# A hybrid mLSTM + Mamba-2 + MoE step on one core: decay exponents moved to ScalarE, a tenth weight slot

## What is computed

```python
def ssd_chunk_scan(x, dt, A, bm, cm, S, chunk):          # the 16 SSD heads
    a = jnp.cumsum(dtc * A[:, None], -1)
    decay = jnp.exp(jnp.where(causal, a[..., :, None] - a[..., None, :], -jnp.inf))
    scores = jnp.einsum('bhtn,bhsn->bhts', cc, bc) * decay * dtc[..., None, :]
    y = jnp.einsum('bhts,bhsp->bhtp', scores, xc) + ...

def hier_moe(x, p):                                      # 16 experts, 12 MB of weights each
    hg = jnp.einsum('sd,edf->sef', xr, p['w_gate'])
    hu = jnp.einsum('sd,edf->sef', xr, p['w_up'])
    return jnp.einsum('sef,efd->sd', jax.nn.silu(hg) * hu * gr[..., None], p['w_down'])
```

## Time and profile before

| what | value |
|---|---|
| median of 3 runs | 798.01 us (796.15 to 798.03) |
| time of the profiled execution | 795.37 us |
| its span in the profile | 793.6 us |
| busy in the span | PE 755.2, DVE 288.3, ACT 213.0, POOL 29.9 us |
| DMA | 263.68 MB, 332 GB/s over the span |
| GB/s in slices of 19.8 us, from 357 us to 754 us | 420 to 433 in each |

### The profile page before, as it was taken

How to read it: one execution, slowest core, us unless ns; L and a number is a source line. 1 busy time by engine, 2 the same in 40 slices (tenths; PEclk the granted TensorE clock), 3 DMA queues, 4 the chain that set the end, 5 groups by cost and what they waited for, 6 DMA issues and landing times.

```text
span 793.6 us, 9613 instructions
## 1 busy us (share of the span) xinstructions
PE 755.2 (95%) x3789; PEld 403.7 (51%) x3789; DVE 288.3 (36%) x699; ACT 213.0 (27%) x598; POOL 29.9 (4%) x90
## 2 busy tenths in 40 slices
PE   6998999998999999999999999999999998998995
PEld 5876888876788887533333333333333332233232
DVE  3943555779989311430031031211300201311204
ACT  4226666738564101611100101001011001001013
POOL 7000000001000100000000000000000000000000
PEclk9999999998999999999999999999999999999998
DMA  9954467756796687779999999999999999999992
GB/s 237 340 186 126 130 211 233 239 186 175 249 294 192 271 321 314 281 287 429 426 429 424 433 420 431 427 423 431 424 429 425 427 425 430 427 427 427 427 399 80
DMA packets 76491, 263.68 MB, mean 332 GB/s; under 512 B 7398, under 2 KB 46570, under 8 KB 62856
## 3 DMA queue, kind: packets, MB, share of 16 engines
q1 hardware_dynamic: 74656, 259.02, 83.6%
q0 software_dynamic: 1568, 3.91, 1.4%
q10 hardware_dynamic: 216, 0.07, 0.1%
HBM read 251.15 MB, written 11.99 MB: 332 GB/s over the span
## 4 chain that ended last, share of the span: by engine, by line
PE 73%; DMA 15%; DVE 7%; ACT 2%; issue 1%; POOL 1%; DVEq 0%; POOLq 0%; ACTq 0%
PE bank L2309 21%; PE bank L1886 10%; PE bank L2388 10%; PE bank L2159 7%; DMA arena<-in_w_down 5%; DMA arena<-in_w_up 5%; DMA ring<-in_w_up 4%; PE bank L1874 4%; PE bank L2334 4%; PE bank L2268 3%; PE bank L1973 2%; DVE h_tok L1425 2%; PE bank L1833 1%; PE bank L2322 1%; PE bank L2278 1%
## 5 line engine op out<-in xcount | busy, mean ns | idle before, releaser
L2309 PE MATMUL bank<-ring,arena 128*64 128x512 f32 x704 | 159.2, 596 | 5.4 <-DMA ring<-in_w_up 3.9
L1886 PE MATMUL bank<-arena,ring 128*128 128x264 f32 (+1 forms) x448 | 110.9, 403 | 5.5 <-DVE arena L1564 2.0
L2309 PEld LDWEIGHTS bank<-ring,arena 128*64 128x64 f32 x704 | 47.9, 137 | 102.4 <-issue 91.0
L1886 PEld LDWEIGHTS bank<-arena,ring 128*128 128x128 f32 x448 | 85.8, 195 | 22.6 <-issue 3.9
L512 DVE COPY arena<-bank 64x512 f32<-64x512 f32 x15 | 10.3, 683 | 205.4 <-PE bank L2388 205.4
L2388 PE MATMUL bank<-ring,arena 128*64 128x512 f32 x304 | 68.1, 593 | 3.0 <-DMA ring<-in_w_down 3.0
L1751 DVE TENSOR_TENSOR arena<-bank,WG 128x512 f32<-128x512 f32 x16 | 16.9, 1056 | 129.7 <-PE bank L2309 129.7
L2159 PE MATMUL bank<-arena,ring 128*128 128x264 f32 x256 | 58.4, 387 | 0.0
L2309 PE MATMUL bank<-arena 128*64 128x512 f32 x240 | 55.6, 598 | 2.0 <-DMA arena<-in_w_up 1.2
L2159 PEld LDWEIGHTS bank<-arena,ring 128*128 128x128 f32 x256 | 48.3, 190 | 8.5 <-issue 0.3
L1218 ACT ACTIVATE arena<-bank 128x512 f32<-128x512 f32 x15 | 9.0, 598 | 148.0 <-PE bank L2322 148.0
(11 more groups left out here) (390 smaller groups left out, 807.4 us busy)
## 6 DMA issues: line engine op xcount, KB each, us to landing
ring<-in_w_gate SPq DMA_DIRECT2D x22, 2048.0 KB, 25.2
ring<-in_w_up SPq DMA_DIRECT2D x22, 2048.0 KB, 28.7
ring<-in_w_down SPq DMA_DIRECT2D x19, 2048.0 KB, 27.4
arena<-in_w_down SPq DMA_DIRECT2D x11, 2048.0 KB, 30.9
ring<-in_w_in SPq DMA_DIRECT2D x9, 2048.0 KB, 9.2
arena<-in_w_up SPq DMA_DIRECT2D x5, 2048.0 KB, 25.5
arena<-in_w_gate SPq DMA_DIRECT2D x5, 2048.0 KB, 31.0
out<-h_tok SPq DMA_DIRECT2D x16, 512.0 KB, 3.6
```

What stands on the lines that cost most here:

```text
L1886: last = mm(b[:, q0:T], slot_k(UNIT_SLOT[u], 512)[:, k, o:o + P], hT[:, k, q0:T], start=(k == 0), stop=(k == KD - 1))
L2309: last = mm(b[CAP * half:CAP * (half + 1), :], XG[:, k, (e % 2) * CAP:(e % 2 + 1) * CAP], w(kk)[:, half * 512:(half + 1) * 512], start=(k ...
```

## The change

It does seven things. (1) For the 16 SSD heads the three argument instructions on DVE are gone. ACT now takes the exponential straight from the spread row, with the head's column as a bias for each partition (`ssd_decay`); since that bias belongs to a block of the 416 columns, it takes three instructions in place of one. What lay beyond the mask is no longer held down by an argument, so DVE's product takes the lower of the exponential and 1 (`decay_weighted`, one instruction as before), and the masked products are set to zero once for each group of 8 heads in PSUM (`causal_products`, three instructions, at `c` = 0 and `c` = 4). (2) SP's reload of a spread row waits for the exponential instead of the arguments. (3) A tenth slot, `spare`, is added; `PLACES` gets it at the fifth place, and its first unit is issued by SP in pass `h` = 5 of the mLSTM loop; the fills of slots that come free later each take the next unit. (4) To make room, `iota_i` and its cast go, three small tiles share one (`NR`), and the memory set aside for descriptors of DMAs is given as 2048 bytes for each partition. (5) POOL's small loads are parted: the last 6 wait for the first two transfers and count on `prev_in`. (6) SP, DVE and PE thus wait for 7 small loads and not 13. (7) Two waits move to where the router weights are used.

```diff
-PLACES = [3, 4, 5, 6, 0, 1, 2, 7, 8]
+PLACES = [3, 4, 5, 6, 8, 0, 1, 2, 7, 9]
...
+        spare = sb("spare", [P, SLOT])
...
-        arrived = unit_in + bb_in + [st_in[2]]
+        arrived = unit_in + bb_in + [x_in[0], st_in[2]]
...
-        slot = [ring[:, i * SLOT:(i + 1) * SLOT] for i in range(6)] + [arena[:, a:a + SLOT] for a in (EARLY, LATE)]
+        slot = [ring[:, i * SLOT:(i + 1) * SLOT] for i in range(6)] + [arena[:, a:a + SLOT] for a in (EARLY, LATE)] + [spare[:, :]]
...
-            sp.wait_ge(s.late_in, 16 * 13)
+            sp.wait_ge(s.late_in, 16 * 7)
             mixer_unit(U_QKV)
...
                     if n >= 4:
-                        sp.wait_ge(s.arg_done, n - 3)
+                        sp.wait_ge(s.arg_done if n < 4 + HA else s.exp_done, n - 3)
...
+                if h == 5:
+                    fill(gate_v, 1, 4)
                 if h == 6:
                     mixer_unit(U_Z + 1)
...
-            first_unit(gate_v, 1, 4, s.wo_unit, 2)
-            first_unit(gate_v, 1, 5, s.wo_unit, 3)
-            first_unit(down_v, 0, 6, s.mo_ps, KD)
+            first_unit(gate_v, 1, 5, s.wo_unit, 2)
+            first_unit(down_v, 0, 6, s.wo_unit, 3)
             first_unit(down_v, 0, 7, s.mo_ps, KD)
             first_unit(up_v, 1, 8, s.mo_ps, KD)
+            first_unit(up_v, 1, 9, s.mo_ps, KD)
...
-            g.iota(iota_i[:], pattern=[[1, P]], base=0, channel_multiplier=0)
+            g.iota(iota[:], pattern=[[1, P]], base=0, channel_multiplier=0, allow_small_or_imprecise_dtypes=True)
...
-            g.tensor_copy(iota[:], iota_i[:])
...
+            pool.wait_ge(s.prev_in, 32)
+            pool.dma_start(wr[:, :, 0:4], w_r1[0].rearrange("(k p) g -> p k g", p=P)).then_inc(s.prev_in, 16)
...
+            def ssd_decay(h):
+
+                if h >= 2:
+                    act.wait_ge(s.y_ps, h - 1)
+                else:
+                    act.wait_ge(s.nc_ps, HA - 1 + h)
+                row = HA + h
+                act.wait_ge(row_in[row % 4], 16 * (row // 4 + 1))
+                for j, q0 in enumerate(Q_FROM):
+                    last = a.activation(ARG[:, h % 2, BLK[j]:BLK[j] + NP - q0], ROWB[row % 4][:, q0:NP], ACT.Exp,
+                                        bias=TM[:, j, 16 + h:17 + h], scale=-1.0)
+                last.then_inc(s.exp_done, 1)
...
             for c in range(KD):
                 if c >= 1:
-                    decay_exp(HA + 2 * c)
-                    decay_exp(HA + 2 * c + 1)
+                    ssd_decay(2 * c)
+                    ssd_decay(2 * c + 1)
...
+            def causal_products(g_):
+
+                for j, q0 in enumerate(Q_FROM):
+                    q1 = min((j + 1) * P, NP)
+                    part = bank[3 + g_][:, BLK[j]:BLK[j] + q1 - q0]
+                    seen = mask[:, q0 - j * P:q1 - j * P] if j < 2 else late[:, 0:16]
+                    last = v.scalar_tensor_tensor(out=part, in0=seen, scalar=0.0, in1=part,
+                                                  op0=ALU.is_equal, op1=ALU.mult)
+                link(last)
...
+                v.scalar_tensor_tensor(out=ARG[:, h % 2, :], in0=ARG[:, h % 2, :], scalar=1.0, in1=b[:, 0:BLKW],
+                                       op0=ALU.min, op1=ALU.mult).then_inc(s.st_done, 1)
...
-                if c + 1 < KD:
-                    ssd_args(2 * c + 2)
-                    ssd_args(2 * c + 3)
                 ssd_out(dve, c)
...
-    nc = _bacc.Bacc("TRN2", target_bir_lowering=False, num_devices=1)
+    nc = _bacc.Bacc("TRN2", target_bir_lowering=False, num_devices=1, dynamic_dma_scratch_size=2048)
```

More of the change, by code:

```diff
@@ L352, in program @@
         m0s = sb("m0s", [HA, NB])
-        N0 = sb("N0", [64, P])
+        NR = sb("NR", [P, P])
+        N0 = NR[0:64, :]
+        N1T = NR[0:64, :]
+        NSTo = NR[64:64 + HA, :]
         N1 = sb("N1", [P, 64])
@@ L423, in unit_at @@
             return UNIT_SLOT[u], sum(48 if n == U_QKV else 16 for n in same)
-        mix_in = [0] * 6 + [64, 64, 16 * len(range(2, HA + NB, 3))]
+        mix_in = [0] * 6 + [64, 64, 16, 16 * len(range(2, HA + NB, 3))]
         for u in range(N_MIX):
@@ L594, in v_rows, with fill @@
                 sp.dma_start(VB[h % 2], v_dram[h:h + 1, :].to_broadcast([P, NB * DH])).then_inc(vb_in[h % 2], 16)
+            gate_v, up_v, down_v = (t[0].rearrange("e (u p k) n -> e u p (k n)", u=2, p=P) for t in (w_gate, w_up, w_down))
+            def fill(w, x, n):
+                i = PLACES[n % NS]
+                if i < len(slot):
+                    sp.dma_start(slot[i], w[x, n % 2]).then_inc(arrived[i], 16)
+                else:
+                    for b in range(2):
+                        sp.dma_start(PIECES[b], w[x, n % 2][:, b * SLOT // 2:(b + 1) * SLOT // 2]).then_inc(arrived[i], 16)
             def state_step(n):
@@ L671, in taken @@
                     sp.wait_ge(s.gu_ps, r * NX + (n + 3) // 6)
[L673 to L680, removed]
             def half_matrix(w, x, n, r):
@@ L691, in first_units @@
                     taken([u for u in range(6 * NX) if u % NS == n][-1], r - 1)
-                    w = (gate_v, gate_v, up_v, up_v, gate_v, gate_v, down_v, down_v, up_v)[n]
-                    fill(w, 1 if n in (4, 5, 8) else 0, n)
+                    w = (gate_v, gate_v, up_v, up_v, gate_v, gate_v, down_v, down_v, up_v, up_v)[n]
+                    fill(w, 1 if n in (4, 5, 8, 9) else 0, n)
             def expert_stream(r):
-                half_matrix(up_v, 1, up_no(1) + 1, r)
                 for x in range(2, NX):
@@ L1037, in _ @@
                     head_in(h + 1)
-                decay_exp(h + 1)
+                if h < HA - 1:
+                    decay_exp(h + 1)
+                else:
+                    ssd_decay(0)
                 if h == HA - 1:
@@ L1085, in _ @@
             z_tanh(0)
-            decay_exp(HA + 1)
+            ssd_decay(1)
             z_tanh(1)
@@ L1404, in _, with decay_args @@
                 .then_inc(s.bcm_ready, 1)
-            def decay_args(n, key):
-                row = n if key < 16 else HA + n
-                b = ROWB[row % 4]
-                dve.wait_ge(row_in[row % 4], 16 * (row // 4 + 1))
+            def decay_args(n):
+                b = ROWB[n % 4]
+                dve.wait_ge(row_in[n % 4], 16 * (n // 4 + 1))
                 for j, t0 in enumerate(S_TILES):
@@ L1476, in _ @@
             dve.wait_ge(s.tm_ready, 1)
[L1477 removed]
+            decay_args(0)
             sample_q_k(0)
@@ L1484, in _ @@
                         dve.wait_ge(s.nc_ps, h)
-                    decay_args(h + 1, h + 1)
-                else:
-                    ssd_args(0)
+                    decay_args(h + 1)
                 c_update(h)
@@ L1557, in pair_weighted @@
                 dve.wait_ge(s.gt_ps, c // 4 + 1)
+                if c % 4 == 0:
+                    causal_products(c // 4)
                 for h in (2 * c, 2 * c + 1):
-                    weighted(HA + h, bank[3 + c // 4])
+                    decay_weighted(h, bank[3 + c // 4])
             def z_out(h):
```

34 lines of the change are left out of this document (11 added, 23 removed).

## The result

The changed kernel took 786.85 us (median of 4 runs, 786.31 to 787.39) beside 797.08 us for the kernel before on the same chip: ratio 0.9873, 95% interval [0.9852, 0.9894]. That is faster, by more than was forecast: 10.2 us between the medians where 7.8 were predicted, and 786.85 lies only 0.35 us above the low edge of the range. The profiled executions say less: 787.24 us with a span of 785.4, against 795.37 and 793.6, thus 8.2 us. Two questions follow: which of the two differences is nearer, and whether each of the four terms of the forecast has its size.

The account below looks back on a forecast made before the run. Last weights were taken to bound the experts, a PE, DVE and ACT chain the part ahead; 0.2 + 0.8 + 1.9 + 4.9 = 7.8 us off 798.0 gave 790.2, range 786.5 to 795.

Parts of the forecast that it names:

- The base: Whole kernel: time before the change taken as 798.0 us, the median of the runs shown, from which 7.8 were subtracted.
- The tenth slot: Expert weight stream: one unit less after the refills start ends it 4.9 us earlier; lower bound 2.7.
- The unit's load: SP's queue near 139 us: the added load delays head 7's values by 4.9 us, at no cost, with 5.6 us of cover.
- `causal_products`: DVE at `c` = 0 and 4: 0.8 us for three instructions, costing nothing; without the cover 1.6.
- Arguments off DVE ahead of the loop: DVE before `c_update` of mLSTM head 7: SSD head 0's arguments go, so the loop starts 0.8 us earlier.
- The loop: SSD passes 1 to 3: arguments moved from DVE to ACT bring pass 4's tile 1.9 us earlier; bounds 0.7 to 2.4.
- The start: Kernel start: without the cast on POOL, PE begins 0.2 us earlier (0 to 0.25); fewer small loads give nothing.
- 1: Experts: the slot gives little, at most 1 us of the 4.9, the stream becoming PE's; 794 us, chance 0.12.
- rival 3: SSD loop: smaller descriptor memory makes POOL wait for its stores, pass 1 12 us later; 802 us; with other losses, chance 0.07.
- Rival 2: SSD loop: ACT takes DVE's place, a pair at 2.5 us or more, loop keeps its length; 792 to 793 us, chance 0.12.
- Rival 4: SSD passes 1 to 3: both PE waits (2.91 + 1.98) go in place of 1.9; 787 us, chance 0.09.
- The signs: Trace marks expected: pass 4's tile at about 215.3, ACT pair 1.9 us, experts some 422 us, weight waits about 4 us.

Follow-up runs that it names:

- nine slots: The changed kernel with the tenth slot taken out again: 792.79 us, ratio 0.9968 to the kernel before.
- big descriptor memory: The changed kernel without the tenth slot and with descriptor memory back at 16384 bytes instead of 2048: 792.14 us, ratio 0.9951 to the kernel before.
- slot only: The changed kernel with the SSD arguments back on DVE, keeping the tenth slot and the new start: 791.15 us, ratio 0.9937 to the kernel before.
- ACT twice: The changed kernel without the tenth slot, with ACT computing the exponentials of heads 2 to 7 twice: 795.87 us (one run).
- The last ACT order: The changed kernel with y_square and first tanh before weighted_x in SSD passes 1-3, square root later, both tanh before pass 3's state decay: 783.80 us, ratio 0.9851.
- late fill: The changed kernel with the tenth slot's first load moved behind two units of wo: 787.88 us, ratio 0.9894 to the kernel before.
- passes 1 to 3: The changed kernel with y_square and the first tanh ahead of weighted_x in three SSD passes, square root later: 786.38 us, ratio 0.9869 to the kernel before.
- the second run of passes 1 and 2: Repeat of the changed kernel with y_square and first tanh ahead of weighted_x in two SSD passes, square root later: 785.52 us, ratio 0.9870.

## Why the prediction was right, term by term

- **The base.** 798.0 was the median of three runs and 2.5 us above the median of 51. With 795.5 the forecast of 7.8 us off gives 787.7; measured 787.3 over ten runs. Made against the profiled execution, as the sum itself was, it stood at 787.6. Against 790.2, as it was put down, 786.85 is 3.4 lower: 2.5 are the base, 0.4 the terms, and 0.5 that these four runs lay under the ten. So it is partly luck that the time fell inside the range; the sizes of the terms are not.
- **The tenth slot, 4.9 us forecast.** 4.92 by the table. The step from "the DMA engines never rest from the first refill on" to "one unit less is one unit's time" held. The Trainium skill (SBUF — State Buffer, the section on a bandwidth-pool intuition that is wrong) gives about 358 GB/s from HBM to one core, by which it would have been 5.9, an estimate; the transfers ran at 427 here, and the measurement decides. Only one sign was off: PE's waits for weights were to fall to 3.8 us and fell to 5.0. The missing 1.2 us are time in which PE is shown busy in the kernel before and not after (from the first expert product, at 339.47 and now 336.07, to e: 426.97 us less 10.9 of waits, and 422.10 less 7.2). A wait costs more than its row shows, as PE's waits in the kernel before tell:

```profile
437.01 3.65 PE L2309 MATMUL bank<-ring,arena 128*64 128x512 f32 x16 [0.72 <-DVE arena L1721]
...
546.35 3.65 PE L2309 MATMUL bank<-ring,arena 128*64 128x512 f32 x16 [0.72 <-DVE arena L1721]
...
619.38 3.65 PE L2309 MATMUL bank<-ring,arena 128*64 128x512 f32 x16 [0.18 <-DMA ring<-in_w_up]
...
656.25 3.66 PE L2309 MATMUL bank<-arena 128*64 128x512 f32 x16 [0.72 <-DVE arena L1721]
```

  From 437.01 to 546.35 there are 109.34 us and no wait for weights (109.35 from 542.96 to 652.31 in the changed kernel, without one either). The next 109.90 hold one of 0.18, which thus cost 0.56. Nine waits for weights became five, and the 1.2 us are 0.29 for each of the four that are gone; that each of them cost as much is not shown.
- **The unit's load.** At no cost, as said: no wait ahead of `c_update` of head 7, and loaded at another place it was worth the same.
- **`causal_products`.** At no cost, as said: pass 4 takes 9.83 us with and without it. The three instructions hold DVE 0.59 us (215.41 to 216.00), where 0.8 were worked out.
- **Arguments off DVE ahead of the loop, 0.8 us.** 0.81 (1.32 against 0.51 us from `weighted` to `c_update`).
- **The loop, 1.9 us forecast (0.7 to 2.4).** 2.2. The mechanism was right: ACT the later engine in passes 1 and 2, the 1.64 us whole in pass 3. The term was mis-sized in pass 1: `weighted_x` was to come 0.1 us earlier beside the loop's start and came 189.31 - 187.76 - 1.20 = 0.35 earlier. ACT was free 0.18 us sooner than worked out (185.96, not 187.34 - 1.20). Half of that is overlap: the next instruction starts 2.34 us behind the start of `decay_state` (183.62), not 2.43. The other 0.09 is chance: `weighted_x` of pass 0 waited 1.23 us and not 1.32 for POOL's stores, and where it waited 1.39 and 1.43 (nine slots, with the small and with the big descriptor memory) t - z is longer by as much, 48.94 and 48.98. Besides, the pair took 1.80 instead of 1.86. This runs on into pass 2, whose `z_out` of tile 4 gained 0.56 (34.13 to 33.57 us behind z) and not 0.2; 0.56 and 1.64 are the 2.2. The price of an exponential with a bias column, drawn from two other rows, was good to 3%.
- **The start, 0.2 us.** 0.25 in PE's first instruction. PE's first projection came 0.5 us earlier, but the rest is no part of the change: eight transposes there took 1.35 us before, 1.10 after and 1.39 in the kernel with nine slots, whose start is the same. That the fewer small loads give nothing fits slot only, which has the whole new start and a z 0.27 us earlier than before (166.94).
- **The rivals.** 1 and 3 fell by experiment. The wait of 1.32 us to which rival 3 points stands ahead of `weighted_x` of pass 0, not of pass 1 as the prediction has it; it was 1.23 us with the small memory. Rival 2 (ACT takes DVE's place) is half true: ACT did so in two passes, and 3.6 us more of ACT there (ACT twice) cost 3.5; at 1.80 us a pair it had not yet eaten the gain of pass 3. Rival 4 (PE loses both waits) did not happen in the changed kernel, which keeps 2.57 and 1.67 us of them; that the time came out at rival 4's 787 is the base and the spread of the runs. The last ACT order goes beyond it: its loop is 5.84 us shorter than before, where both waits are 4.89.
- **The signs.** The tile of pass 4 was to begin at about 215.3 and began at 214.79; `weighted_x` of pass 1 was to gain at most 0.3 us and gained 0.35; a pair was to hold ACT 1.9 us and held it 1.80; some 422 us from the first expert product to PE's last wait were 422.10.

## What to carry to other kernels

Cut the time line at marks where one engine's start is fixed by another, and compare the pieces: here t - z and e - r agreed to 0.4 us or better between kernels that share the part, where the intervals of the ratios are 3 to 5 us wide. Where transfers run without a gap from a first refill to the end, and the consumer has waits to give up, price one more buffer at one unit's transfer time: here 4.92 us for a unit of 4.91, from either of the two places ahead where it was loaded. After work has moved from one engine to another, look at what the new one does first: an instruction that waits for a load, or that nobody needs yet, in front of one that two engines wait for cost 3.6 us here, more than the move itself gave (0.8 + 2.2).

## What the runs showed of the hardware

Executions of the kernel before spread over 7 us in 51 runs. Where two traces that should be alike differ by 0.8 us or more in a piece, PE's granted clock differs in a window of it. Four of the twelve traces of the table had 0.83 in the window from 10 to 20 us and the other eight 1.00, all behind a first idle of PE of 5.3 to 5.5 us: late fill, big descriptor memory, passes 1 to 3, and the second run of passes 1 and 2. They are the four whose z lies at 167.28 or later; for the ten-slot kernels with the exponents on ACT that is 2.0 to 2.9 us behind the others (165.74 to 166.01). In one of them (passes 1 to 3) 16 products that elsewhere take 4.00 us at 13.46 took

```profile
14.20 5.53 PE L1883 MATMUL bank<-arena,WG 128*80 128x280 f32 x16 [1.05 <-DVE bank L1333]
```

The earliest z (ACT twice, 164.85) goes the other way: it had 1.00 from 70 to 80 us, where the kernel with nine slots had 0.83, and 16 products took 4.04 us at 74.07 in place of 5.73 at 73.75. A dip between 320 and 340 us, in three traces, adds 0.8 to 1.0 to r - t (125.7 to 126.5 and more). A dip inside the SSD loop cost nothing where PE would have waited for DVE anyway (slot only). The programs that are compared do the same at these places, and why the clock falls in one execution and not in another stays open. So a difference of 2 us between two single executions of this kernel says nothing until the windows have been looked at.
